# Scatter products between the gate and up products of the next expert pair

## What is computed

```python
def moe(h, router_w, router_b, wg, wu, wd):
    B, T, D = h.shape
    x = h.reshape(B * T, D)
    scores = jax.nn.sigmoid((x @ router_w).astype(jnp.float32))
    ...
    hid = jax.nn.silu(jnp.einsum('nd,edf->nef', x, wg)) * jnp.einsum('nd,edf->nef', x, wu)
    y = jnp.einsum('nef,efd->nd', hid * combine[..., None].astype(hid.dtype), wd)
    return y.reshape(B, T, D)
```

## Time and profile before

| | us |
|---|---|
| median of 3 runs | 1899.71 |
| lowest, highest of them | 1898.18, 1908.43 |
| the profiled execution | 1896.61 |
| its span, first to last instruction | 1894.8 |
| TensorE busy in it | 1778.0 |
| VectorE, ScalarE busy | 476.2, 386.1 |

### The profile page before, as it was taken

How to read it: one execution, slowest core, us unless ns; L and a number is a source line. 1 busy time by engine, 2 the same in 40 slices (tenths; PEclk the granted TensorE clock), 3 DMA queues, 4 the chain that set the end, 5 groups by cost and what they waited for, 6 DMA issues and landing times.

```text
span 1894.8 us, 21657 instructions
## 1 busy us (share of the span) xinstructions
PE 1778.0 (94%) x8808; PEld 1051.2 (55%) x8808; DVE 476.2 (25%) x1240; ACT 386.1 (20%) x775; POOL 40.6 (2%) x52
## 2 busy tenths in 40 slices
PE   4999999999998979999998999999998999999986
PEld 2677544346635867844444657844444778444443
DVE  0242411115200251321112244431111344211102
ACT  1232200003102561200002224300001342000002
POOL 1000000000000000000000000000000000000000
PEclk8999999999998988999999999999999999999988
DMA  9979699997997325489999786689999457899960
GB/s 323 351 287 385 265 423 426 428 413 257 355 358 265 133 95 186 168 343 427 427 428 398 271 318 260 246 343 428 426 427 405 146 220 283 353 427 426 428 292 22
DMA packets 134022, 609.46 MB, mean 322 GB/s; under 512 B 12486, under 2 KB 19278, under 8 KB 108961
## 3 DMA queue, kind: packets, MB, share of 16 engines
q1 hardware_dynamic: 116880, 589.32, 78.2%
q10 hardware_dynamic: 12528, 10.70, 1.8%
q0 software_dynamic: 4512, 8.02, 1.1%
HBM read 606.15 MB, written 8.92 MB: 325 GB/s over the span
## 4 chain that ended last, share of the span: by engine, by line
PE 77%; DMA 15%; DVE 3%; ACT 3%; issue 1%; ACTq 0%; DVEq 0%; SPq 0%; POOLq 0%
PE PS L962 22%; PE PS L1536 18%; PE PS L1547 9%; DMA arena<-in_moe_wu 7%; PE PS L1500 6%; DMA arena<-in_moe_wg 6%; PE PS L992 4%; PE PS L1044 3%; PE PS L1012 2%; PE PS L1480 1%; DMA arena<-token_rows,IDX 1%; PE PS L1513 1%; DMA ring<-in_w_mod 1%; PE PS L1030 1%; DVE RS L1674 1%
## 5 line engine op out<-in xcount | busy, mean ns | idle before, releaser
L1536 PE MATMUL PS<-ring,arena 128*64 128x512 f32 x1312 | 393.3, 606 | 12.6 <-DMA arena<-in_moe_wu 6.1
L893 ACT ACTIVATE arena<-PS 128x512 f32<-128x512 f32 (+2 forms) x131 | 71.4, 545 | 825.0 <-PE PS L1527 335.0
L1536 PEld LDWEIGHTS PS<-ring,arena 128*64 128x64 f32 x1312 | 125.3, 140 | 204.8 <-issue 204.8
L2063 DVE TENSOR_TENSOR arena<-arena,PS 128x512 f32<-128x512 f32 x32 | 33.5, 1046 | 585.7 <-PE PS L1536 585.7
L962 PE MATMUL PS<-HS,ring 128*128 128x256 f32 x768 | 175.6, 387 | 4.6 <-ACT arena L729 3.0
L1536 PE MATMUL PS<-arena 128*64 128x512 f32 x576 | 169.4, 594 | 1.2 <-DMA arena<-in_moe_wg 1.2
L962 PEld LDWEIGHTS PS<-HS,ring 128*128 128x128 f32 x768 | 146.7, 194 | 31.1 <-issue 8.6
L1500 PE MATMUL PS<-arena 128*128 128x256 f32 (+3 forms) x688 | 143.7, 365 | 10.3 <-ACT arena L893 4.3
L1547 PE MATMUL PS<-ring,arena 128*64 128x512 f32 x656 | 148.8, 596 | 0.5 <-DVE arena L2044 0.5
L1500 PEld LDWEIGHTS PS<-arena 128*128 128x128 f32 (+1 forms) x688 | 117.8, 194 | 51.1 <-issue 22.7
L962 PE MATMUL PS<-arena,ring 128*128 128x256 f32 x640 | 140.5, 382 | 2.5 <-ACT arena L659 1.1
(11 more groups left out here) (334 smaller groups left out, 1687.9 us busy)
## 6 DMA issues: line engine op xcount, KB each, us to landing
ring<-in_w_mod SPq DMA_DIRECT2D x48, 2048.0 KB, 16.1
ring<-in_moe_wu SPq DMA_DIRECT2D x41, 2048.0 KB, 22.9
ring<-in_moe_wd SPq DMA_DIRECT2D x41, 2048.0 KB, 21.9
ring<-in_moe_wg SPq DMA_DIRECT2D x41, 2048.0 KB, 23.1
arena<-in_moe_wg SPq DMA_DIRECT2D x24, 2048.0 KB, 21.1
HS<-in_moe_wu SPq DMA_DIRECT2D x12, 2048.0 KB, 18.8
arena<-in_moe_wu SPq DMA_DIRECT2D x12, 2048.0 KB, 22.7
arena<-in_moe_wd SPq DMA_DIRECT2D x12, 2048.0 KB, 27.3
```

Source lines behind the costliest of these rows:

```text
L893: A(dst, src, func).then_inc(S(sem), 1)
L1536: ins = mm(PS[64 * e:64 * e + 64, b, :], XG[:, k, 64 * e:64 * e + 64], w[:, k], start=(k == 0), stop=(k == KD - 1))
L2063: tt(by_k(HID), row(SG), row(bank(here[1])), ALU.mult).then_inc(S("hid"), 1)
```

## The change

The eight scatter products of a pair are split. Products 0 to 5 move from behind up to between gate and up, with their wait for `ys` (and, in pair 1, for `idx`). Products 6 and 7, the last of which raises `scatter`, move behind the feature turn. The row turn, with its wait for the rows, moves ahead of the feature turn and its wait for `hid`. In pair 0 the order stays as it was.

```diff
-                def scatter(par, sem, first=False, rows=P):
-                    for t in range(8):
+                def scatter(par, sem, first=False, ts=range(8), rows=P):
+                    for t in ts:
                         ins = pick(bank(t // 2, N2 * (t % 2), N2 * (t % 2) + N2), YS[0:rows, P * t:P * t + P], WTS[0:rows, par, 0:N2],
                                    first and t % 2 == 0, True)
-                    ins.then_inc(S(sem), 1)
+                    if t == 7:
+                        ins.then_inc(S(sem), 1)
...
+                    def turned_rows():
+
+                        pe.wait_ge(S(f"slot_rows{1 - par}"), 8 * i + (48 * l + 8 if par else 64 * l + 16))
+                        turn_x(there, 1 - par, "gather")
+
                     for g in range(2):
                         ws = [landed(pe, n0 + 6 * i + 2 * g + e) for e in range(2)]
                         up(ws, here[g], "up", 2 * n + 2 if g == 0 else None)
                         if first and g == 0:
                             slot_id()
-                    if isinstance(i, int) and i == 1:
-                        pe.wait_ge(S("idx"), l + 1)
-                    if not first:
-                        pe.wait_ge(S("ys"), 2 * n)
-                        scatter(1 - par, "scatter", first=(i == 1))
+                        if not first and g == 0:
+                            if i == 1:
+                                pe.wait_ge(S("idx"), l + 1)
+                            pe.wait_ge(S("ys"), 2 * n)
+                            scatter(1 - par, "scatter", first=(i == 1), ts=range(6))
+                    if more and not first:
+                        turned_rows()
                     pe.wait_ge(S("hid"), n + 1)
                     turn_h(here[0], "turn_h")
+                    if not first:
+                        scatter(1 - par, "scatter", first=(i == 1), ts=range(6, 8))
                     if more:
                         pe.wait_ge(S("pw"), 4 * n + (4 * l + 12))
                         turn_w(here[1], "turn_w")
-                        pe.wait_ge(S(f"slot_rows{1 - par}"), 8 * i + (48 * l + 8 if par else 64 * l + 16))
-                        turn_x(there, 1 - par, "gather")
+                    if more and first:
+                        turned_rows()
                     pe.wait_ge(S("hts"), n + 1)
```

## The result

| | before | after |
|---|---|---|
| median, us | 1900.56 (13 runs) | 1888.74 (13 runs) |
| lowest, highest | 1897.95, 1908.43 | 1884.17, 1896.96 |
| profiled execution, its span | 1896.61, 1894.8 | 1884.17, 1882.4 |

The ratio is 0.9933 (95% interval 0.9916 to 0.9951), 9 to 16 us less. In two further comparisons of the same two kernels it was 0.9963 (0.9944 to 0.9983) and 0.9936 (0.9911 to 0.9961). The forecast was a gain of 5.5 us, less than 0.5%; the kernel gained about twice that. The median, 1888.74 us, still lies just inside the forecast range of 1888.5 to 1900.5, but that is luck: no case behind the range gained more than 8.9 us, and its lower end came from the spread of medians.

The account below looks back on a forecast made before the run. DMA was taken to bound the expert pairs. Gain 8.9 us in pair 7 over four layers, less two clock falls of 1.7, is 5.5; from the median 1899.71 that gives 1894.2 us, range 1888.5 to 1900.5.

Parts of the forecast that it names:

- What bounds the kernel: Expert pairs of the MoE stages: DMA is slower, 29.4 us a pair against 25.9 of TensorE.
- The term that pays: Pair 7, after the last wu chunk lands: down starts at 414.2 instead of 416.48, 2.2 us a layer, 8.9 in four.
- Up of pair 7 starts on time: Pair 7: gate and six scatter products end by 404.4, so up still starts at its landing, 404.45, nothing to spare.
- The middle pairs: Pairs 1 to 6: each grows from 25.9 to 26.2, perhaps 26.3 us; waits for DMA swallow the lateness.
- What is late next, the clock: Ahead of gate of pair 7: a 2.2 to 2.7 us wait, two clock falls in four layers, 1.7 us lost each.
- no clock fall: Rival, wait ahead of gate of pair 7: clock stays up in all layers, gain 8.9, time 1890.8 us; chance 0.13.
- The base: Kernel before, pair 6: a clock fall after the 2.7 us wait in each of four layers, costing nothing there.
- It can't be more: End of the MoE stages: gain limited to 2.2 us a layer, 8.9 in four, while chunks land when they do.
- From the profiled execution to the median: Whole kernel: median 1899.71 is 3.1 us above the profiled execution; the same gain taken from it gives 1894.2.
- What else is moved: Later loads behind up, earlier row turn, added wait for ys: each costs 0; the gain passes through the next mixer.
- The slower rival: Pairs 1 to 3: later end of up leaves the DMA queue empty, 12.5 us more, 1912.2; chance 0.06.
- The rule of the Trainium skill: Wait ahead of gate of pair 7: by the 3 us rule alone it costs nothing, sum 8.9 us; trace disagrees.

Follow-up runs that it names:

- the experiment with short middle pairs: Against the kernel before, only pairs 6 and 7 got the new order, pairs 1 to 5 kept the old one; ratio 0.997, stages 791.9 us.

## Why the prediction was wrong

The forecast, 1894.2 us, was a gain of 5.5 us; the medians say 11.8, the stages 10.0. By its own steps:

- **What bounds the kernel: right.** The landings of the chunks set the end. The last wd chunk of layer 0, issued at 383.0 in the changed kernel, took 30.2 us to land, as before:

```profile
L468 SPq DMA_DIRECT2D HS<-in_moe_wd x1: 327/327/327, 383.0 to 383.0; - x1
...
DMA to landing us min/median/max: 30.2/30.2/30.2
```

- **The term that pays: right.** 2.2 us from up to down in pair 7 (12.03 less 9.83), with 1.19 us idle ahead of the feature turn and none for the copy, and down starting within 0.2 us of wd's landing (413.2). Between the first two traces the four stages differ by 8.2 us; 8.9 was worked out.
- **Up of pair 7 starts on time: right**, with gate at its landing and nothing to spare (403.55).
- **The middle pairs: under-sized.** "From 25.9 to 26.2, perhaps 26.3"; it was 26.65. I had counted the open wait (0.24 measured, 0.3 worked out) but moved every step at the duration that it had in its old place. In the new order most steps took some hundredths more (0.44 to 0.50 for the feature turn, 0.21 to 0.31 for the weight turn); why was not tested. The forecast said that up of pair 6 would start "at its landing or 0.4 later"; in the three traces of the changed kernel it started 0.8 to 3.0 us after the landing. (The 3.0 are of a layer in which pair 0 had also waited 1.59 us for rows.)
- **What is late next, the clock: the step that failed.** "A wait of 2.2 to 2.7 us therefore stands ahead of gate of pair 7", and "I take two falls in four layers". The wait was 0 to 1.9 us in twelve layers, and there was no fall. The lateness of pair 6 had used the wait up, 0.4 us more than forecast in each of five middle pairs: in each of the nine layers that still have a wait, the delay of up of pair 6 behind its landing and the wait add up to 2.7 us. The two falls had taken 3.4 us off the forecast. The mechanism itself is no error: in the experiment with short middle pairs the wait was 2.55 us, and two falls in four layers cost 1.7 and 1.4 us. The rival "no clock fall" (gain 8.9) came nearest; it had 0.13.
- **The base: a second error, smaller and hidden.** The sum was made against one execution in which the clock had fallen in pair 6 in all four layers, where it is free, and I held that for a property of the kernel ("in each of the four layers"). In 3 of 12 layers of before the fall is in pair 7 and costs 1.3 to 1.6 us; the change removes these too. These three falls are 4.6 us, 1.5 for each execution. They make most of the way from 8.2 to 10.0; the rest I put down to landings that differ by up to 1.4 us between executions, which is not shown. "It can't be more" was wrong for the same reason.
- **From the profiled execution to the median: right in kind.** The profiled executions of both kernels were among their fastest, 4.0 and 4.6 us below the medians.
- **What else is moved: right.** The loads behind up were issued later (249.7 for the wd chunk of pair 1 that was 248.2 before, in an execution that was 1.6 us ahead) and landed in their turn; no wait for rows, `ys` or `idx` appeared in pairs 1 to 7 (the one wait for rows in the three traces of the changed kernel, 1.59 us, is in pair 0, whose order is as before); the gain passed through the mixers.
- **The slower rival** did not come, the DMA share stayed at 1.0. A slower version exists nearby, though, and I had not named it: the same split without the row turn moved up.
- **The rule of the Trainium skill** (page "TensorE: Matmul & The Clock Gate", section "Why this matters for your kernels"), no idle gaps over about 3 us, would have given 8.9 us here. It came nearer than my two falls, but not for its reason: gaps of 2.55 and 2.70 us, below its figure, did bring falls in these kernels, and the change left none of them.

## What to carry to other kernels

Where a stage is bound by a stream of loads, count only the work that stands behind the last landings: move other work ahead of it, or cut the last loads so that half of their work can start earlier; here, cutting the chunks of one pair in eight gave as much as the reordering (10.2 and 10.0 us), and both together, with the order changed in the last two pairs alone, 23.6. Slack elsewhere is spent freely, but it is finite: measure how far the middle of the loop may grow. When steps are moved, allow them more than they took in their old place, and before trusting a clock fall or its absence in one trace, look at a second: behind waits of 2.5 to 2.7 us the falls changed place from execution to execution.

## What the runs showed of the hardware

- The granted clock fell behind 17 of 23 waits of 2.7 us and behind 2 of 4 of 2.55 us, and behind none of the 32 waits for a chunk of 1.0 to 2.42 us inside the stages. A fall made the gate or up behind the wait take 1.3 to 1.7 us longer. The same wait in the same place was followed by a fall in one execution and not in the next.
- Chunks of 2048 KB that were issued ahead landed one each 4.89 us with one expert's rows of 16 KB in a partition's part, and one each 4.95 to 5.0 us with two experts' rows of 8 KB each.
- Between executions of one kernel, the time outside the four stages varied by up to 19 us, that inside them by 3.
- Something else brought a fall more surely than those waits. Between gate and up of pair 0 stand 28 matmul instructions of one column each (L1522), 3.3 to 4.2 us of them. In 47 of the 48 layers traced the clock fell with them or right behind them, and up of pair 0 took 8.3 to 9.9 us instead of 6.9. This lies ahead of the stages, and that up takes 8.9 us on the mean of twelve layers in both kernels, so it has no part in the 10.0 us. Whether the time could be won was not tested: it may come back as a wait for the chunks. Layer 0 of before, on the timeline and in the clock of a stretch:

```profile
212.38 3.29 PE L1522 MATMUL PS<-consts,arena 128*128 128x1 f32 x28
...
216.37 1.06 PE L1536 MATMUL PS<-HS,arena 128*64 128x512 f32 x1
...
215.00:225.00 10.00, 9.38 (x39) 3.20 (x38) 0.85 (x3) 1.88 (x2) 2.08 (x2) 0.83 0.96 408
```
